# A two-stage transformer kernel: row gathers in loops with listed indices, and row products that read the tokens from PSUM

## The chip, the cores and the metric

One core of one Trainium2 chip runs the whole program. The metric is the device time of one execution in microseconds (us), given as the median of several runs. Everything is computed in float32.

## The reference, cut to what matters

Two blocks run one after the other on 256 tokens of width 1024. The first has two layers of attention and a wide MLP. The second has two layers, each a mixer (sparse attention "nsa", then forgetting attention "fox") and a feed-forward made of experts that are single rows:

```python
def peer_ffn(x, w_q, sub_keys, u, v):
    # 8 heads; each picks 16 of 128 x 128 experts by two top-16 searches
    ...
    h = jax.nn.gelu(jnp.einsum('ted,td->te', u[ec], xc))
    return jnp.einsum('te,ted->td', gc.astype(h.dtype) * h, v[ec])
```

`u` and `v` have 16384 rows of 1024 numbers. Each token uses 8 x 16 = 128 of them, so `ec` has the shape (tokens, 128). The dot of a token with its row of `u` gives a weight, and the rows of `v` are summed with these weights.

## The kernel before, in words

The tokens lie on the 128 partitions in two tiles, t = 0 and 1. The first block, and the start of the second, are a sequence of stages (`SCHEDULE`) that end about 900 us after the start; their weights stream through a ring of two panels of 2 MB.

The rest of the program is the **gather phase**. It has four windows (`WINDOWS`: layer 0 tile 0, layer 0 tile 1, layer 1 tile 0, layer 1 tile 1), each of 128 slots: a slot is one expert of each of 128 tokens. Four slots make a tick (`SLICE`), so a window has 32 ticks (`TICKS`) and the phase has 128. For every slot:

- GpSimd (POOL) gathers one row of `u` for each partition with an indirect DMA (L2262), 128 rows of 4 KB, into one of eight buffers (`urow`, `RING` = 8), and in the same way one row of `v` into one of eight buffers `vrow`. The loop at L2303 to L2310 is written out: it issues u of tick n + 1, then v of tick n. A gather into a buffer in use waits for the count `u_used` or `v_used` (L2261). The first gather of a piece of experts waits for `routed`, which VectorE steps at L1890.
- VectorE (DVE) multiplies the landed u row with the tokens `xn` and sums the product (`expert_dots`, L1917). The result goes to `hdot`, and `u_used` rises by one.
- ScalarE (ACT) applies the gelu to four dots (L1370), multiplies them by the gates (L1375) and spreads each over a diagonal matrix (L1381).
- TensorE (PE) multiplies this diagonal with the v row and adds it up in PSUM banks 0 and 1 (`expert_slice`, L906), and `v_used` rises by one. At a window's end VectorE adds the two banks to the residual (`fold`, L1926) and normalizes (L1931, L1941).

Beside this, the mixer of the next tile or layer and its routing are computed in small steps. `STAGES` gives each stage the tick at which it begins, and the plans (`nsa_plan`, `fox_plan`, `LATE_ROUTE`) give each step a tick. On each engine a step of tick n stands behind the expert work of tick n, so all orders are fixed by hand. A step that uses PSUM is named by a letter and a number: S (scores, softened by DVE at L1968 and L1973 and made to exponentials by ACT at L1454), P (shares turned by PE, L972), O (shares times values, L981), q, k, v, w (projections, L926), s (key scores). They take the banks 2 to 7 in turn:

```python
return ps[:, 8 - SHADOW_BANKS + NUMBER[key] % SHADOW_BANKS, :]
```

and PE waits before it fills a bank until the step six places earlier has been read (`bank`, L885). The softmax works in a buffer `soft` in `scratch`, with `softT` for its transpose. For tile 0 two batches of four heads have room in it, for tile 1 one (`block_of`: depth 2 or 1), so for tile 1 `soften` waits until the batch before has been turned (L1966).

A head is ranked by DVE in `rank_head` (L1839 to L1867) and the experts are written in `choose` (L1873 to L1890). In the first window the first two heads are ranked before tick 0, and gathers begin once the first is chosen; the others are ranked between the dots of ticks 0 to 6.

## Time and profile before

| | |
|---|---|
| median of 3 runs | 2522.19 us (2518.62 to 2525.67) |
| the profiled execution | 2530.18 us, of which 2528.1 us span |
| granted TensorE clock, mean | 0.931 of full speed |
| busy in the span | PE 2149.1 us, DVE 1415.3, ACT 880.9, POOL 1155.1 |
| moved by DMA | 754.69 MB, 544.05 of them by POOL's queue |

An engine's busy time counts its instructions, not what it waits for. For a gather the POOL's time is that in which it makes the transfer's descriptors; the transfer itself runs on the 16 DMA engines and is counted there. The DMA share of a window is the mean busy share of these engines; GB/s is what they moved.

In a row of a timeline stand the start and the duration in us, the engine, the line, the operation with what it writes and reads, and in brackets how long the engine was idle before and who released it ("issue": nothing that the profile shows; "remote": unknown).

### The profile page before, as it was taken

What the parts mean: (1) busy time and instruction counts of PE and PEld (TensorE: products, weight loads), DVE (VectorE), ACT (ScalarE), POOL (GpSimd) and SP (SyncE); (2) the same over time, 40 slices, a digit from 0 to 9 for tenths busy, and PEclk for the clock granted to TensorE, in tenths of its full rate; (3) what the DMA queues carried; (4) which work ended last, traced back from release to release, by engine and by line L of the source; (5) the groups of instructions that cost most, each with busy time, mean ns of one, the idle gap of its engine ahead of it and who ended that gap; (6) DMA issues with size and microseconds to landing.
All of it is one profiled execution on the core that took longest, in us unless ns stands there. A gap on an engine that the chain in (4) does not pass through costs nothing.

```text
span 2528.1 us, 24194 instructions
## 1 busy us (share of the span) xinstructions
PE 2149.1 (85%) x7260; PEld 1254.8 (50%) x7260; DVE 1415.3 (56%) x2996; ACT 880.9 (35%) x2125; POOL 1155.1 (46%) x1076
## 2 busy tenths in 40 slices
PE   7889999799999876798977998887798898667776
PEld 5667878678876542453433444343345343222232
DVE  3474554554565468674575644486635466674433
ACT  3445444644534321462222252233234223222121
POOL 0100000000000047687667667767667767777765
PEclk9999999899999799899999999998899899988898
DMA  8315545055445389899999999999999999999997
GB/s 302 146 67 183 191 174 186 31 175 195 170 146 204 113 327 353 287 338 405 415 409 371 409 410 344 413 413 398 371 414 342 377 412 368 361 323 369 378 354 299
DMA packets 172681, 754.69 MB, mean 299 GB/s; under 512 B 19184, under 2 KB 19344, under 8 KB 152736
## 3 DMA queue, kind: packets, MB, share of 16 engines
q0 software_dynamic: 148640, 544.05, 56.3%
q1 hardware_dynamic: 21584, 197.14, 21.0%
q10 hardware_dynamic: 2352, 12.24, 1.3%
q8 instruction: 49, 0.80, 0.1%
q14 instruction: 56, 0.46, 0.1%
HBM read 752.28 MB, written 4.22 MB: 299 GB/s over the span
## 4 chain that ended last, share of the span: by engine, by line
PE 51%; POOL 12%; DVE 11%; issue 10%; DMA 9%; ACT 3%; another core or an unknown queue 3%; DVEq 1%; ACTq 0%; POOLq 0%; SPq 0%
PE ps L906 15%; POOL Z L2262 12%; PE ps L651 7%; PE ps L652 7%; PE ps L653 7%; PE ps L926 7%; DMA Z<-v,experts 5%; DVE Z L1917 4%; DMA Z<-u,experts 3%; DMA ring<-panels 1%; PE ps L1046 1%; DVE ring_lo L1748 1%; PE ps L641 1%; PE ps L981 1%
## 5 line engine op out<-in xcount | busy, mean ns | idle before, releaser
L906 PE MATMUL ps<-Z 128*128 128x512 f32 x2048 | 995.7, 642 | 259.7 <-DMA Z<-v,experts 175.8
L906 PEld LDWEIGHTS ps<-Z 128*128 128x128 f32 x2048 | 410.0, 206 | 808.1 <-issue 566.3
L1917 DVE CUSTOM_DVE_ANT_0 Z<-Z,xn 128x1024 f32<-128x1024 f32 x512 | 609.6, 1225 | 311.8 <-DMA Z<-u,experts 256.7
L2262 POOL DMA_INDIRECT Z<-u,experts x512 | 561.9, 1097 | 329.1 <-issue 157.3
L2262 POOL DMA_INDIRECT Z<-v,experts x512 | 569.3, 1112 | 262.8 <-issue 126.0
L1748 DVE TENSOR_TENSOR ring_lo<-ring,ring_hi 128x1024 fp32r<-128x1024 f32 x212 | 247.6, 1221 | 195.1 <-ACT ring_hi L1212 194.8
L926 PE MATMUL ps<-ring,o 128*128 128x512 f32 x560 | 251.9, 602 | 2.7 <-issue 1.9
L651 PE MATMUL ps<-ring_hi,xT_lo 128*128 128x512 f32 x592 | 237.4, 401 | 13.7 <-DVE xT_lo L1796 7.3
L652 PE MATMUL ps<-ring_lo,xT 128*128 128x512 f32 x592 | 233.0, 394 | 0.0
L653 PE MATMUL ps<-ring_hi,xT 128*128 128x512 f32 x592 | 232.8, 393 | 0.0
L1212 ACT CAST ring_hi<-ring 128x1024 fp32r<-128x1024 f32 x212 | 208.9, 1051 | 37.8 <-DMA ring<-panels 35.2
L1370 ACT ACTIVATE hdot<-hdot 128x4 f32<-128x4 f32 x128 | 26.5, 207 | 536.3 <-DVE hdot L1917 328.9
L2251 POOL COPY Z<-pj 128x256 f32 x16 | 6.4, 402 | 413.9 <-ACTq L524 365.8
L1381 ACT ACTIVATE Z<-cst,wslot 128x128 f32<-128x128 f32 x512 | 165.3, 392 | 64.1 <-PE ps L906 31.3
L926 PEld LDWEIGHTS ps<-ring,o 128*128 128x128 f32 x560 | 106.8, 193 | 133.6 <-issue 132.6
L2297 POOL COPY ksc<-pj 128x512 f32<-128x512 f32 x5 | 3.4, 712 | 304.1 <-DVE pj L1836 298.1
L651 PEld LDWEIGHTS ps<-ring_hi,xT_lo 128*128 128x128 f32 x592 | 112.6, 190 | 44.9 <-DVE ring_lo L1748 9.4
L653 PEld LDWEIGHTS ps<-ring_hi,xT 128*128 128x128 f32 x592 | 112.6, 190 | 23.9
L652 PEld LDWEIGHTS ps<-ring_lo,xT 128*128 128x128 f32 x592 | 112.8, 191 | 22.9 <-issue 0.5
L1375 ACT ACTIVATE wslot<-hdot,gate_w 128x1 f32<-128x1 f32 x512 | 109.6, 285 | 9.1 <-issue 0.3
L651 PE MATMUL ps<-ring_hi,hT 128*128 128x512 f32 x256 | 100.5, 393 | 1.7 <-DVE hT L1756 1.5
L1389 ACT COPY scratch<-ps 128x512 f32<-128x512 f32 (+1 forms) x70 | 38.5, 568 | 180.4 <-PE ps L926 82.8
(262 smaller groups left out, 2025.6 us busy)
## 6 DMA issues: line engine op xcount, KB each, us to landing
ring<-panels SPq DMA_DIRECT2D x106, 1024.0 KB, 5.0
ring<-panels SPq DMA_DIRECT2D x40, 2048.0 KB
Z<-u,experts POOLq DMA_INDIRECT x512
Z<-v,experts POOLq DMA_INDIRECT x512
gain<-gains ACTq DMA_DIRECT2D x4, 1024.0 KB, 4.5
pj<-keys ACTq DMA_DIRECT2D x4, 1024.0 KB
bias_lines<-bias_line POOLq DMA_DIRECT2D x1, 3072.0 KB, 17.2
gain<-gains ACTq DMA_DIRECT2D x5, 512.0 KB, 3.6
```

Of the source, the lines that this page charges most:

```text
L651: mm(out, b, c, start=start, stop=False)
L652: mm(out, a, d, start=False, stop=False)
L653: return mm(out, a, c, start=False, stop=stop)
L906: last = mm(ps[:, c, :], diag[s], vrow[s][:, c * NC:(c + 1) * NC], start=slot == 0, stop=slot == SLOTS - 1)
L926: last = mm(to, tokT[:, k, :], w[:, k * NC:(k + 1) * NC], start=k == 0, stop=k == KT - 1)
L1212: copy(ring_hi[:, slot, c * CH:(c + 1) * CH], ring[:, slot, c * CH:(c + 1) * CH]).then_inc(hi_ready, 1)
L1375: f(own[:, s:s + 1], cols[:, s:s + 1], ACT.Copy, scale=gate_w[:, t, slot + s:slot + s + 1])
L1381: f(diag[n % RING], ident, ACT.Copy, scale=own[:, s:s + 1]).then_inc(diag_ready, 1)
L1389: copy(to, src).then_inc(act_emptied, 1)
L1748: v.tensor_tensor(ring_lo[:, slot, at], ring[:, slot, at], ring_hi[:, slot, at].bitcast(F32), ALU.subtract).then_inc(lo_ready, 1)
L1917: v.tensor_tensor_reduce(out=urow[s], in0=urow[s], in1=xn[:, t, :], scale=1.0, scalar=0.0, op0=ALU.mult, op1=ALU.add, accum_out=hdot[:, t, ...
L2262: g.indirect_dma_start(out=rows[s], out_offset=None, in_=tables[layer], in_offset=bass.IndirectOffsetOnAxis(ap=experts[:, t, slot:slot + 1 ...
```

## The change

Four things change; the arithmetic is the same.

1. The u dots read the tokens from PSUM. At the start of each window DVE copies the tile's tokens into banks 6 and 7 (`dotted`), and L1917 takes them from there as its second operand.
2. The steps beside the gathers therefore have four banks (2 to 5), from the end of the "middle" stage on; that stage keeps six. For tile 1, `ksc` gives a second buffer for `soft` and `softT`, so that both tiles have depth 2.
3. DVE copies the four indices of each tick into one of four short lists (`listed`), two ticks ahead, behind the dots (`list_rows`). From the fifth tick on it first waits for the v rows that used the list before. Gathers read the lists instead of `experts`, and wait for `rows_listed` instead of `routed`.
4. POOL issues the first four ticks written out (`first_rows`), and then runs a loop whose body is 32 gathers, for four ticks of u and of v. The loop makes 15 turns for each layer, with one such body written out between the two, where u comes from layer 1 and the first v still from layer 0. In these 992 gathers each wait is an instruction of its own (`apart`), against a value computed from the loop's register.

The diff, cut to its core:

```diff
...
-SHADOW_BANKS = 6
+FRONT_BANKS, SHADOW_BANKS = range(2, 8), range(2, 6)
...
+N_MIDDLE = sum(key[0] == "middle" for key in ORDER)
+BANK = [FRONT_BANKS[n % len(FRONT_BANKS)] if n < N_MIDDLE else SHADOW_BANKS[n % len(SHADOW_BANKS)]
+        for n in range(len(ORDER))]
...
+LISTS, LISTED_AHEAD = 4, 2
...
+        listed = sb("listed", [P, LISTS, SLICE], U32)
...
+        dotted = ps[:, 6:8, :]
...
-            return ps[:, 8 - SHADOW_BANKS + NUMBER[key] % SHADOW_BANKS, :]
+            return ps[:, BANK[NUMBER[key]], :]
...
-            t = 0 if key[0] in ("middle", "fox0") else 1
-            return t, int(key[1][1]), (1, 2)[t == 0]
+            return 0 if key[0] in ("middle", "fox0") else 1, int(key[1][1]), 2
...
+            n = BATCH * (t + 1) * P
+            a = (soft, ksc_flat[:, 0:BATCH * SEQ])[i % 2] if t == 1 else soft[:, i % 2 * n:]
+            return a[:, 0:n]
...
+        def soft_turned(key):
+            t, i, depth = block_of(key)
+            n = BATCH * (t + 1)
+            a = (softT, over(ksc_flat[:, BATCH * SEQ:], [[P, 2 * BATCH], [1, P]]))[i % 2] if t == 1 else softT[:, i % 2 * n:]
+            return a[:, 0:n]
...
-                n = NUMBER[key]
-                if n >= SHADOW_BANKS:
-                    emptied(pe, ORDER[n - SHADOW_BANKS])
+                last = held_before(NUMBER[key], BANK[NUMBER[key]])
+                if last is not None:
+                    emptied(pe, ORDER[last])
...
             def expert_dots(tick):

                 t = tick // TICKS % TILES
+                if tick == 0:
+                    for b in (6, 7):
+                        emptied(dve, ORDER[held_before(len(ORDER), b)])
+                if tick % TICKS == 0:
+                    dve.drain()
+                    for c in range(2):
+                        v.tensor_copy(dotted[:, c, :], xn[:, t, c * NC:(c + 1) * NC])
+                    dve.drain()
                 for n in range(tick * SLICE, (tick + 1) * SLICE):
                     s, slot = n % RING, n % SLOTS
                     dve.wait_ge(u_landed[s], 16 * (n // RING + 1))
-                    v.tensor_tensor_reduce(out=urow[s], in0=urow[s], in1=xn[:, t, :], scale=1.0, scalar=0.0,
+                    row = over(urow[s], [[NC, 2], [1, NC]])
+                    v.tensor_tensor_reduce(out=row, in0=row, in1=dotted, scale=1.0, scalar=0.0,
                                            op0=ALU.mult, op1=ALU.add, accum_out=hdot[:, t, slot:slot + 1])\
                         .then_inc(u_used, 1)
+
+            def list_rows(tick):
+
+                t, at = tick // TICKS % TILES, tick % TICKS * SLICE
+                if tick >= LISTS:
+                    for n in range((tick - LISTS) * SLICE, (tick - LISTS + 1) * SLICE):
+                        dve.wait_ge(v_landed[n % RING], 16 * (n // RING + 1))
+                v.tensor_copy(listed[:, tick % LISTS], experts[:, t, at:at + SLICE]).then_inc(rows_listed, 1)

...
                     phase()
             steps = Ticks(beside())
             steps.upto(-1)
+            for tick in range(LISTED_AHEAD):
+                list_rows(tick)
             for tick in range(len(WINDOWS) * TICKS):
                 expert_dots(tick)
+                if tick + LISTED_AHEAD < len(WINDOWS) * TICKS:
+                    list_rows(tick + LISTED_AHEAD)
                 steps.upto(tick)
...
-            def gather(rows, tables, there, tick):
-
-                layer, t = WINDOWS[tick // TICKS]
+            def u_rows(layer, tick, place):
+
+                apart(pool, (rows_listed, tick + 1))
+                for b in range(SLICE):
+                    s = (place * SLICE + b) % RING
+                    apart(pool, (u_used, tick * SLICE + (b + 1 - RING)))
+                    g.indirect_dma_start(out=urow[s], out_offset=None, in_=(u0, u1)[layer],
+                                         in_offset=bass.IndirectOffsetOnAxis(ap=listed[:, place, b:b + 1], axis=0))\
+                        .then_inc(u_landed[s], 16)
+
+            def v_rows(layer, tick, place):
+
+                for b in range(SLICE):
+                    s = (place * SLICE + b) % RING
+                    apart(pool, (v_used, tick * SLICE + (b + 1 - RING)))
+                    g.indirect_dma_start(out=vrow[s], out_offset=None, in_=(v0, v1)[layer],
+                                         in_offset=bass.IndirectOffsetOnAxis(ap=listed[:, place, b:b + 1], axis=0))\
+                        .then_inc(v_landed[s], 16)
...
                 for n in range(tick * SLICE, (tick + 1) * SLICE):
-                    s, slot = n % RING, n % SLOTS
                     if n >= RING:
                         pool.wait_ge(u_used if rows is urow else v_used, n - RING + 1)
-                    g.indirect_dma_start(out=rows[s], out_offset=None, in_=tables[layer],
-                                         in_offset=bass.IndirectOffsetOnAxis(ap=experts[:, t, slot:slot + 1], axis=0))\
-                        .then_inc(there[s], 16)
+                    g.indirect_dma_start(out=rows[n % RING], out_offset=None, in_=table,
+                                         in_offset=bass.IndirectOffsetOnAxis(
+                                             ap=listed[:, tick, n % SLICE:n % SLICE + 1], axis=0))\
+                        .then_inc(there[n % RING], 16)

             for (step, arg), meets in zip(SCHEDULE, MEETS):
...
-            for tick in range(-1, len(WINDOWS) * TICKS):
-
-                after = tick + 1
-                if after < len(WINDOWS) * TICKS:
-                    pool.wait_ge(routed, piece_of(after // TICKS, after % TICKS * SLICE))
-                    gather(urow, (u0, u1), u_landed, after)
-                if tick >= 0:
-                    gather(vrow, (v0, v1), v_landed, tick)
+            for tick in range(LISTS):
+                pool.wait_ge(rows_listed, tick + 1)
+                first_rows(urow, u0, u_landed, tick)
+                if tick > 0:
+                    first_rows(vrow, v0, v_landed, tick - 1)
+            turn = TILES * TICKS // LISTS
+            with pool.Fori(1, turn) as i:
+                for k in range(LISTS):
+                    u_rows(0, i * LISTS + k, k)
+                    v_rows(0, i * LISTS + (k - 1), (k - 1) % LISTS)
+            for k in range(LISTS):
+                u_rows(1, turn * LISTS + k, k)
+                v_rows(k > 0, turn * LISTS + k - 1, (k - 1) % LISTS)
+            with pool.Fori(turn + 1, 2 * turn) as i:
+                for k in range(LISTS):
+                    u_rows(1, i * LISTS + k, k)
+                    v_rows(1, i * LISTS + (k - 1), (k - 1) % LISTS)
+            v_rows(1, 2 * turn * LISTS - 1, LISTS - 1)
```


## Rows read from the trace of the kernel before

**Rows 1.** Windows: length, busy PE, PEld, DVE, ACT, POOL (instructions), clock, DMA share, GB/s
```profile
1000.00:1100.00 100.00, 82.62 (x302) 45.55 (x301) 70.92 (x151) 51.63 (x143) 68.25 (x59) 0.88 0.86 304
1100.00:1200.00 100.00, 83.44 (x239) 39.48 (x237) 55.38 (x113) 34.82 (x104) 76.25 (x68) 0.93 0.99 381
1200.00:1300.00 100.00, 89.36 (x244) 42.49 (x245) 62.48 (x178) 27.63 (x87) 67.36 (x64) 0.98 1.02 413
1300.00:1400.00 100.00, 74.77 (x170) 31.72 (x169) 59.75 (x143) 24.62 (x80) 71.00 (x66) 0.89 1.00 385
...
1500.00:1600.00 100.00, 80.06 (x208) 37.75 (x207) 48.65 (x91) 31.49 (x100) 72.81 (x63) 0.90 0.96 368
...
1700.00:1800.00 100.00, 71.68 (x157) 32.35 (x158) 61.58 (x148) 24.43 (x80) 71.22 (x68) 0.84 1.00 386
1800.00:1900.00 100.00, 100.00 (x271) 47.58 (x270) 53.23 (x132) 34.88 (x93) 63.23 (x55) 0.99 1.01 403
1900.00:2000.00 100.00, 87.25 (x283) 45.22 (x281) 53.99 (x99) 39.24 (x115) 72.10 (x64) 0.95 0.93 346
2000.00:2100.00 100.00, 93.62 (x249) 44.03 (x250) 61.44 (x177) 25.76 (x85) 67.67 (x62) 0.95 1.02 411
2100.00:2200.00 100.00, 72.76 (x145) 29.51 (x143) 63.30 (x148) 27.36 (x89) 77.96 (x70) 0.90 0.96 359
2200.00:2300.00 100.00, 68.75 (x130) 27.61 (x131) 63.31 (x144) 22.08 (x78) 74.83 (x66) 0.85 0.93 341
2300.00:2400.00 100.00, 72.44 (x144) 29.22 (x142) 43.20 (x70) 20.89 (x79) 69.99 (x72) 0.90 0.97 371
2400.00:2528.00 128.00, 88.46 (x176) 35.62 (x176) 50.39 (x86) 25.43 (x93) 75.50 (x76) 0.90 0.87 328
```

**Rows 2.** Groups by line: busy us, mean ns | idle before, releaser
```profile
L1917 DVE CUSTOM_DVE_ANT_0 Z<-Z,xn 128x1024 f32<-128x1024 f32 x512 | 609.6, 1225 | 311.8 <-DMA Z<-u,experts 256.7
L2262 POOL DMA_INDIRECT Z<-u,experts x512 | 561.9, 1097 | 329.1 <-issue 157.3
L2262 POOL DMA_INDIRECT Z<-v,experts x512 | 569.3, 1112 | 262.8 <-issue 126.0
```

**Rows 3.** Timeline, 1341 to 1347 us: GpSimd beside VectorE
```profile
1341.77 1.23 DVE L1926 TENSOR_TENSOR h<-ps,h 128x1024 f32<-128x1024 f32 x1 [5.10 <-remote]
...
1342.01 0.94 POOL L2262 DMA_INDIRECT Z<-v,experts  x1 [3.29 <-remote]
...
1343.13 1.23 DVE L1931 CUSTOM_DVE_ANT_0 o<-h 128x1024 f32<-128x1024 f32 x1
1343.25 1.92 POOL L2262 DMA_INDIRECT Z<-u,experts  x1 [0.31 <-issue]
```

**Rows 4.** Timeline, POOL where the gathers begin
```profile
901.82 1.02 POOL L2262 DMA_INDIRECT Z<-u,experts  x1 [113.79 <-DVE experts L1890]
...
923.83 1.18 POOL L2262 DMA_INDIRECT Z<-u,experts  x1 [7.27 <-DVE hdot L1917]
```

**Rows 5.** Timeline, DVE where the gathers begin
```profile
921.82 1.23 DVE L1917 CUSTOM_DVE_ANT_0 Z<-Z,xn 128x1024 f32<-128x1024 f32 x1
...
922.97 1.22 DVE L1917 CUSTOM_DVE_ANT_0 Z<-Z,xn 128x1024 f32<-128x1024 f32 x1
```

**Rows 6.** Chain that ended last: start us, us, what
```profile
2503.93 4.48 DMA Z<-v,experts
```

**Rows 7.** Waits of POOL from 930 us: us in total, times, longest us
```profile
POOL Z L2262 <- DVE hdot L1917: 54.3, 16, 8.1
```

**Rows 8.** Timeline, POOL copies beside a turn of a loop
```profile
95.98 0.39 POOL L2252 COPY Z<-pj 128x256 f32 x1
96.32 0.40 POOL L2251 COPY Z<-pj 128x256 f32 x1
```

**Rows 9.** Waits of DVE from 900 us
```profile
DVE scratch L1968 <- PE ps L972: 23.6, 8, 4.6
```

**Rows 10.** Timeline, DVE among the steps that rank a head
```profile
977.24 0.43 DVE L1851 TENSOR_TENSOR ranks<-ranks 128x256 f32<-128x256 f32 x1 [2.34 <-issue]
```

More of the change, by code:

```diff
@@ L130, with held_before @@
 NUMBER = {key: n for n, key in enumerate(ORDER)}
+N_MIDDLE = sum(key[0] == "middle" for key in ORDER)
+BANK = [FRONT_BANKS[n % len(FRONT_BANKS)] if n < N_MIDDLE else SHADOW_BANKS[n % len(SHADOW_BANKS)]
+        for n in range(len(ORDER))]
+def held_before(n, bank):
+    return max((m for m in range(n) if BANK[m] == bank), default=None)
 def by_dve(key):
@@ L505, in build @@
         routed = sem("routed")
+        rows_listed = sem("rows_listed")
         logits_ready = sem("logits_ready")
@@ L969, in turn_shares @@
                 pe.wait_ge(soft_ready, softened(key))
-                to, at = bank(key), soft_at(key) + BATCH * P * "ab".index(key[1][2])
+                to, at = bank(key), BATCH * P * "ab".index(key[1][2])
                 for j in range(BATCH):
-                    last = tr(to[:, j * P:(j + 1) * P], soft[:, at + j * P:at + (j + 1) * P], ident)
+                    last = tr(to[:, j * P:(j + 1) * P], soft_of(key)[:, at + j * P:at + (j + 1) * P], ident)
                 last.then_inc(bank_filled, 1)
@@ L977, in weigh @@
                 emptied(pe, (key[0], in_batch("P", t, i)[-1]))
-                to, at = bank(key), soft_at(key) // P
+                to = bank(key)
                 for j in range(BATCH):
                     for kb in range(t + 1):
-                        last = mm(to[:, j * HD:(j + 1) * HD], softT[:, at + j * (t + 1) + kb, :], values[j][kb],
+                        last = mm(to[:, j * HD:(j + 1) * HD], soft_turned(key)[:, j * (t + 1) + kb, :], values[j][kb],
                                   start=kb == 0, stop=kb == t)
@@ L1441, in copy_shares @@
                     filled(act, (key[0], f"O{i - depth}"))
-                at = soft_at(key) // P + 4 * "ab".index(key[1][2])
-                copy_bank(key, softT[:, at:at + 4, :], fours(key))
+                at = 4 * "ab".index(key[1][2])
+                copy_bank(key, soft_turned(key)[:, at:at + 4, :], fours(key))
             def soft_exps(stage, i):
@@ L1452, in soft_exps @@
                 for j in range(BATCH):
-                    a = soft[:, at + j * keys_of:at + (j + 1) * keys_of]
+                    a = soft_of(key)[:, j * keys_of:(j + 1) * keys_of]
                     last = f(a, a, ACT.Exp, bias=peaks[i % 2][:, j:j + 1], accum_out=totals[i % 2][:, j:j + 1])
@@ L1963, in soften @@
                 m, heads = "ab".index(key[1][2]), BATCH // 2
-                a = over(soft[:, soft_at(key) + m * keys_of:], [[2 * keys_of, heads], [1, keys_of]])
+                a = over(soft_of(key)[:, m * keys_of:], [[2 * keys_of, heads], [1, keys_of]])
                 if i >= depth:
@@ L2253, in stage_pairs, with first_rows @@
                         last.then_inc(staged, 1)
[L2255 to L2257 removed]
+            def u_rows(layer, tick, place):
[13 more added lines that the diff above has]
+                        .then_inc(v_landed[s], 16)
+            def first_rows(rows, table, there, tick):
                 for n in range(tick * SLICE, (tick + 1) * SLICE):
[L2259 removed]
                     if n >= RING:
                         pool.wait_ge(u_used if rows is urow else v_used, n - RING + 1)
[L2262 to L2264 removed]
+                    g.indirect_dma_start(out=rows[n % RING], out_offset=None, in_=table,
+                                         in_offset=bass.IndirectOffsetOnAxis(
+                                             ap=listed[:, tick, n % SLICE:n % SLICE + 1], axis=0))\
+                        .then_inc(there[n % RING], 16)
             for (step, arg), meets in zip(SCHEDULE, MEETS):
```

6 lines of the change are left out of this document (3 added, 3 removed).

## The prediction

> **What bounds the kernel now.** I read the windows first, then the groups by line, then the timeline of GpSimd beside VectorE, and last the waits.
>
> The kernel has two halves. The change touches only the second, from the first row gather, some 900 us after the start, to the end at 2528.1. In it 1024 gathers bring 512 KB each (128 rows of 4 KB), u and v in turn. The windows [rows 1] show that no engine is full there: PE is busy 69 to 100 us in 100, DVE 43 to 71, POOL 63 to 78. The column to read is the last one. It goes between two levels: 411 to 413 GB/s in four windows (1200, 1400, 1600 and 2000; first and last stand in the rows), where weight panels come beside the gathers, and 304 to 403 in the others. So the DMA engines can take 412, and in the lower windows they are not given enough.
>
> Who gives them too little is in the groups [rows 2]. A gather costs POOL 1097 to 1112 ns and "issue" before it. The timeline [rows 3] says what its floor is: 0.94 us of work and 0.30 us before the next, 1.245 us from start to start, which would be 0.524 MB / 1.245 us = 421 GB/s, just above what DMA takes. But many gathers last up to 1.99 us. Rows 3 show when: the gather at 1342.01 runs wholly beside L1926, a DVE addition of the same 1024 columns that reads one operand from PSUM and one from SBUF, and takes 0.94 us. The next one, at 1343.25, runs beside L1931, a product with a sum that reads SBUF twice, and takes 1.92 us. L1917, the dot of a u row, is of the form of L1931, and there are 512 of them. A gather that meets one waits until it is through. Over 1024 gathers this is 561.9 + 569.3 - 1024 x 0.945 = 163.5 us of POOL [rows 2].
>
> **Part 1: dots with the tokens in PSUM.** The second SBUF operand goes, so a gather should cost 0.945 us always, like the one at 1342.01 [rows 3]. What this is worth is limited in each window by two numbers of rows 1: the POOL time set free (its busy time less count x 0.945), and the room in DMA, 100 us x (1 - GB/s / 412). I take the smaller:
> 1000: 12.5 (room 26); 1100: 7.5 (freed 12.0); 1300: 6.5 (freed 8.6); 1500: 10.7 (freed 13.3); 1700: 6.3 (freed 7.0); 1900: 11.6; 2100: 11.8; 2200: 12.5; 2300: 2.0; 2400 to 2528: 3.7. The four full windows give 0, and 1800 gives 0 because PE is busy 100.00 of it. Sum 85.1 us.
>
> The dot's own length: L1926 takes 1.23 us for 1024 columns with one operand in PSUM, L1917 1.225, so 0. If it did grow by a tenth, 512 x 0.12 = 61 us would fall on DVE, which idles 311.8 us before its dots, 256.7 of them for the very rows [rows 2]; that cover hides most of it. Nothing shorter than 0.94 us stands in any row, so I allow no gain beyond it.
>
> The tokens must be copied to PSUM at four window starts: two copies of 512 columns and two drains. L1926's 1.23 us for 1024 columns bounds a copy from above; with drains I take 2 us each, 8 in all, half of it hidden by rows in flight: 4 us.
>
> **Part 2: index lists and loops.** Each tick DVE copies four indices into a list, after four waits on v rows. Those v rows were issued before the u rows whose dots have just run, so the waits pass at once. No row shows such a copy; it lies between 0 and one dot (1.225 us), nearer to 0: I take 0.5 us with its waits. 128 of them are 64 us of DVE, hidden by the 256.7 us that it waits for u rows. That cover is missing in the first eight ticks, where DVE ranks heads between dots: 4 us.
>
> **Start.** Before, the first gather left at 901.82, as soon as the first experts were written, and POOL then stood idle 7.27 us [rows 4] for the first dot, at 921.82 [rows 5]. Now the list is written where the first dot stood. The first dot needs the copy (0.5), the wake-up of POOL (0.78: the dot at 921.82 ends at 923.05 and the gather it releases starts at 923.83, [rows 4, 5]), 0.94 for the gather and its landing. A landing takes 4.48 us in the last links of the chain [rows 6]. Together 6.7 us, all on the path, since DVE ranks heads and is the slowest there.
>
> **Coarser release.** Before, row n of u waited for dot n - 8 alone. Now a slice of four waits for the list, that is for all four dots of two slices before. When POOL stands at that point, it waits up to 3 x 1.15 + 0.5 = 3.9 us longer (dots start 1.15 us apart, [rows 5]). POOL waited for DVE 16 times, 54.3 us [rows 7]; 16 x 3.9 = 62 us is the most, 0 the least (if the rows in flight cover it). About half of those waits lie in stretches where DMA has a queue: 31 us.
>
> Loop control: each gather gets a separate wait against a register, a semaphore step, and arithmetic. The POOL copies of L2251 and L2252 already run in such a loop, one on each side of a turn, and stand 0.34 us apart [rows 8], with nothing in between. A gather gives the sequencer 1.245 us. I take 0; what it would cost if not hidden is a rival.
>
> **Part 3: four banks, two soft buffers.** In a tick of attention for tile 1 five steps fill a bank (Sa, Sb, O, Pa, Pb), so PE's fifth waits for the first to be read by DVE. DVE mostly stands waiting for PE at that place, as rows 9 show, so this is near 0. On the other side, DVE no longer waits until the previous batch is turned: L1968 waited for PE L972 8 times, 23.6 us [rows 9]. A third of that reaches POOL: +8 us. Bounds: -24 (the last rival) to +24.
>
> **Sum.** 85.1 - 4 - 4 - 6.7 - 31 + 8 = 47.4 us. The profiled execution took 2530.18 us (span 2528.1), so 2482.8; it lies 8.0 above the median of the three runs, 2522.19, so **2475 us**.
>
> A limit from elsewhere: the Trainium skill, "DMA: Bandwidth & Descriptors", section Bandwidth, says that one core's share of HBM is about 358 GB/s and binds for loads. By it the windows would have no room and the sum would be a loss of about 38 us. The trace disagrees with 413 GB/s over 100 us [rows 1], and the measurement decides.
>
> **Rivals.**
> - *The freed time comes whole* (0.17). The release costs nothing because a faster POOL keeps a deeper queue. 85.1 + 8 - 14.7 = 78, and more where room exceeds what was freed (1000, 1900, 2200): 2425 to 2445.
> - *Gathers alone cannot reach 412* (0.10). The DMA share is 0.93 to 1.00 in windows of 341 to 386 GB/s too [rows 1]; perhaps scattered rows are slower than panels. With 386 as ceiling the 85.1 fall to about 54 (1000: 12.5; 1100 and 1300: 1.6; 1500: 4.7; 1700: 0; 1900: 10.4; 2100: 7.0; 2200: 11.7; 2300 and 2400: 5.7), less the same 38 us of costs: 16 us gained, 2506, and up to 2530 when the costs run high, as no queue of rows covers them here: mostly 2515 to 2525. Against it: 385 and 386 are also just what the POOL gives at 1.49 to 1.52 us per gather.
> - *The loop's control shows between gathers* (0.10), the slower side. If a separate wait is passed only when the gather ahead has left, the 0.78 us of a wake-up [rows 4, 5] stand in place of 0.30. On the 992 gathers issued this way that is up to 476 us. It decides from 0.05 us per gather on, 47 us over 992: above that the kernel is slower. Likely size if it happens: 0.06 to 0.15 us, 2535 to 2625. Against it stand the copies, 0.34 us apart across a turn [rows 8]. A variant is one code load per turn of the loop: DVE stands "issue" 2.34 us in a row of small instructions at 977.24 with nothing to wait for [rows 10]; 30 turns x 2.34 = 70 us, which gives 2545. The Trainium skill, "Runtime: NRT & Kernel Launch", section Instruction fetch mechanics, says that a taken branch to a place outside the two loaded blocks forces a fetch. By that rule it hangs on the length of the body, 32 gathers with their waits, which no row here shows.
> - *Four banks hold PE up* (0.03): a stall of 2 us in each of some 12 ticks with five banks, 24 us, and POOL waits for v slots: 2500.
>
> **How the numbers follow.** The forecast's own range is 2455 to 2505, with 0.60. About 0.3% (7.6 us) is what a measurement of this kernel can tell from no change. Faster: 0.58 of the forecast's 0.60 (the rest for its upper edge), 0.17 and 0.03 of the first and last rivals: 0.78. Same: that edge, 0.02, and 0.08 of the second rival. Slower: 0.10 of the third and 0.02 of the second. The range takes in the first rival's likely part, the second, and the near edge of the third: 2425 to 2530.
>
> **What would show it.** Right: gathers of 0.94 us on average (POOL busy near 970 us, not 1131), no gather of 1.99 us beside a dot, windows 2100 to 2400 near 385 to 405 GB/s, the first gather after 922, POOL's wait for DVE up from 54 to 80 or 100 us, dots still 1.22 us. Wrong: gathers still of 1.9 us; gaps of 0.4 us or more between gathers with no releaser; windows without panels that stay below 390 GB/s while POOL stands waiting for used slots.

## The result and the profile after

The changed kernel takes 2579.68 us (median of 4 runs, 2570.94 to 2588.15) against 2520.40 of the kernel before beside it: a ratio of 1.0234 [1.0194, 1.0274], 59 us slower, where 47 us faster was predicted. In a later session it gave 1.0227 [1.021, 1.0244]. On a chip on which the kernel before itself takes only 2451.54 us, the same kernel was 0.9917 [0.9901, 0.9934], 18 us **faster**. Both belong to the result. The experiments below explain the loss; why that chip turns it into a gain stays open in part.

The groups by line of the kernel after (profiled execution 2588.15 us, span 2586.0), which answer to [rows 2]:

```profile
L1949 DVE CUSTOM_DVE_ANT_0 Z<-Z,ps 128x1024 f32<-128x1024 f32 x512 | 607.7, 1219 | 293.6 <-DMA Z<-u,listed 227.6
L2305 POOL DMA_INDIRECT Z<-u,listed x496 | 475.7, 959 | 342.7 <-DVE listed L1959 189.2
L2314 POOL DMA_INDIRECT Z<-v,listed x500 | 474.7, 949 | 310.3 <-issue 141.9
```

The gathers fell from 1097 to 1112 ns to 949 to 959, and the dots kept their length. Beside a dot a gather now takes 0.94 us, where [rows 3] had 1.92. Two dots in VectorE's timeline of the kernel after:

```profile
1345.34 1.22 DVE L1949 CUSTOM_DVE_ANT_0 Z<-Z,ps 128x1024 f32<-128x1024 f32 x1
...
1346.48 1.22 DVE L1949 CUSTOM_DVE_ANT_0 Z<-Z,ps 128x1024 f32<-128x1024 f32 x1
```

and the gathers beside them, in GpSimd's:

```profile
1345.92 0.94 POOL L2314 DMA_INDIRECT Z<-v,listed  x1 [2.88 <-remote]
1347.16 0.94 POOL L2314 DMA_INDIRECT Z<-v,listed  x1 [0.30 <-issue]
```

So the first step of the forecast holds: POOL got its time back (busy 1001.6 us, before 1155.1). But it could not use it. The windows, in the columns of [rows 1]:

```profile
1000.00:1100.00 100.00, 69.89 (x226) 35.34 (x225) 66.78 (x163) 38.07 (x110) 55.78 (x57) 0.85 0.80 295
1100.00:1200.00 100.00, 75.55 (x255) 39.49 (x253) 53.91 (x122) 38.08 (x105) 49.97 (x54) 0.86 0.75 284
1200.00:1300.00 100.00, 90.01 (x210) 40.47 (x211) 43.83 (x100) 25.87 (x84) 57.06 (x60) 0.91 1.02 413
...
2200.00:2300.00 100.00, 66.20 (x128) 27.15 (x127) 66.11 (x199) 21.31 (x74) 60.20 (x63) 0.85 0.92 338
2300.00:2400.00 100.00, 68.97 (x140) 28.05 (x138) 52.61 (x93) 25.48 (x88) 64.87 (x69) 0.90 0.95 362
```

The window from 1100 had 68 gathers and 381 GB/s, and now has 54 and 284. The two late ones shown, which were to rise to 385 or more, stay at 338 and 362 (the one from 2100 rose from 359 to 380). POOL stood waiting instead. Its waits from 930 us on (us in total, times, longest us), which answer to the one row of [rows 7]:

```profile
POOL Z L2305 <- DVE listed L1959: 189.2, 34, 11.7
POOL Z L2305 <- issue: 148.5, 449, 3.8
POOL Z L2314 <- issue: 141.9, 419, 3.5
POOL Z L2314 <- remote: 85.0, 25, 5.5
POOL Z L2314 <- PE ps L929: 80.6, 47, 4.2
```

The 189.2 us for the lists stand where 54.3 us for dots stood before. "issue" is mostly the 0.30 us ahead of every gather. One of the long waits, first in VectorE's timeline:

```profile
1104.77 0.69 DVE L2008 SCALAR_TENSOR_TENSOR scratch<-ps,cst 128x512 f32<-128x512 f32 x1 [6.36 <-remote]
...
1107.42 1.22 DVE L1949 CUSTOM_DVE_ANT_0 Z<-Z,ps 128x1024 f32<-128x1024 f32 x1
...
1110.84 1.22 DVE L1949 CUSTOM_DVE_ANT_0 Z<-Z,ps 128x1024 f32<-128x1024 f32 x1
...
1111.98 0.17 DVE L1959 COPY listed<-experts 128x4 uint32<-128x4 uint32 x1
```

and in GpSimd's:

```profile
1100.45 0.94 POOL L2314 DMA_INDIRECT Z<-v,listed  x1 [0.30 <-issue]
1113.12 0.94 POOL L2305 DMA_INDIRECT Z<-u,listed  x1 [11.73 <-DVE listed L1959]
```

DVE is held up for 6.36 us at a soften of the attention beside ("remote": the trace does not say by whom), then does four dots, and only then copies the list. A gather that waits for its slot alone goes when the first of those dots is done, at 1108.6; this one goes at 1113.12. Meanwhile 11.7 us pass without a new row, and the DMA engines run dry. In the columns of [rows 1], the last 6 us of the wait are:

```profile
1107.00:1113.00 6.00, 5.45 (x34) 3.57 (x33) 5.91 (x14) 5.74 (x17) 0.00 (x0) 1.00 0.01 3
```

They moved 3 GB/s there.

### The profile page after: what moved, and what is told of

Its sections match the earlier page's. It is cut to its first block, busy times and chain, and to the rows that moved or that the text cites. A ratio compares the mean times of both kernels' runs of the same rounds, so it can differ in the third digit from the quotient of the medians.

```text
span 2586.0 us, 26357 instructions
## 1 busy us (share of the span) xinstructions
PE 2161.2 (84%) x7260; PEld 1258.0 (49%) x7260; DVE 1427.4 (55%) x3132; ACT 880.2 (34%) x2125; POOL 1001.6 (39%) x1076
## 4 chain that ended last, share of the span: by engine, by line
PE 41%; issue 15%; DVE 14%; DMA 11%; POOL 8%; another core or an unknown queue 5%; ACT 3%; DVEq 2%; POOLq 1%; ACTq 0%; SPq 0%
PE ps L929 9%; PE ps L674 7%; PE ps L675 7%; PE ps L676 7%; DMA Z<-v,listed 7%; DVE Z L1949 6%; PE ps L949 5%; POOL Z L2305 4%; POOL Z L2314 3%; DMA Z<-u,listed 3%; DMA ring<-panels 1%; PE ps L1069 1%; DVE ring_lo L1771 1%; PE ps L664 1%
## 5 line engine op out<-in xcount | busy, mean ns | idle before, releaser
L929 PE MATMUL ps<-Z 128*128 128x512 f32 x2048 | 1009.3, 648 | 288.0 <-DMA Z<-v,listed 155.3
L1949 DVE CUSTOM_DVE_ANT_0 Z<-Z,ps 128x1024 f32<-128x1024 f32 x512 | 607.7, 1219 | 293.6 <-DMA Z<-u,listed 227.6
L2305 POOL DMA_INDIRECT Z<-u,listed x496 | 475.7, 959 | 342.7 <-DVE listed L1959 189.2
L2314 POOL DMA_INDIRECT Z<-v,listed x500 | 474.7, 949 | 310.3 <-issue 141.9
L674 PE MATMUL ps<-ring_hi,hT 128*128 128x512 f32 x256 | 100.4, 392 | 1.6 <-DVE hT L1779 1.5
L676 PE MATMUL ps<-ring_hi,hT 128*128 128x512 f32 x256 | 99.7, 390 | 0.0
```

What stands on the lines that cost most here:

```text
L674: mm(out, b, c, start=start, stop=False)
L676: return mm(out, a, c, start=False, stop=stop)
L929: last = mm(ps[:, c, :], diag[s], vrow[s][:, c * NC:(c + 1) * NC], start=slot == 0, stop=slot == SLOTS - 1)
L1949: v.tensor_tensor_reduce(out=row, in0=row, in1=dotted, scale=1.0, scalar=0.0, op0=ALU.mult, op1=ALU.add, accum_out=hdot[:, t, slot:slot + 1])\
L2305: g.indirect_dma_start(out=urow[s], out_offset=None, in_=(u0, u1)[layer], in_offset=bass.IndirectOffsetOnAxis(ap=listed[:, place, b:b + 1] ...
L2314: g.indirect_dma_start(out=vrow[s], out_offset=None, in_=(v0, v1)[layer], in_offset=bass.IndirectOffsetOnAxis(ap=listed[:, place, b:b + 1] ...
```

## The experiments

The ratios are against the kernel before of the same session, which took 2511 to 2522 us except where noted. There were five such sessions, on four chips; the chip of the first measurement is not on record.

**Banks and soft buffers alone.** The changed kernel without lists, without loops, and with the dots from SBUF:

```diff
-SHADOW_BANKS = 6
+FRONT_BANKS, SHADOW_BANKS = range(2, 8), range(2, 6)
...
-            return t, int(key[1][1]), (1, 2)[t == 0]
+            return 0 if key[0] in ("middle", "fox0") else 1, int(key[1][1]), 2
```

> The kernel before with four banks and two soft buffers alone; the dots read SBUF, gathers as before. Theory A: within 10 us of before, 2510 to 2530. Rival B: 2550 or more.

2511.03 us, 0.9996 [0.9967, 1.0025], as theory A has it. Part 3 costs nothing.

**PSUM dots with them.** The same with the dots of the change; the gathers read `experts` as before.

```diff
-                    v.tensor_tensor_reduce(out=urow[s], in0=urow[s], in1=xn[:, t, :], scale=1.0, scalar=0.0,
+                    row = over(urow[s], [[NC, 2], [1, NC]])
+                    v.tensor_tensor_reduce(out=row, in0=row, in1=dotted, scale=1.0, scalar=0.0,
```

> The changed kernel with the lists and the loops taken out: gathers written out as before, reading experts, each waiting for one slot; the dots still read PSUM, four banks, two soft buffers. Theory A (the loss is the list: POOL waits for four dots and a copy instead of one dot, 189 us behind L1959 now): POOL's waits fall back to about 54 us behind DVE and the time to 2450 to 2500 us, below the kernel before. Rival B (the four banks and the faster POOL make PE and DVE wait for each other): the time stays at 2550 to 2580.

2500.19 us, 0.9966 [0.9941, 0.999], and 0.9952 [0.993, 0.9973] in a session on another chip. So the PSUM dots gain 11 us over the kernel just above. The time lies at the upper edge of theory A, and the waits for dots came to 103.8 us and not to 54. The groups and waits of both say where the rest stays. The groups of GpSimd with dots from SBUF (kernel with banks alone):

```profile
L2293 POOL DMA_INDIRECT Z<-u,experts x512 | 549.6, 1073 | 338.3 <-issue 150.6
L2293 POOL DMA_INDIRECT Z<-v,experts x512 | 557.6, 1089 | 268.9 <-issue 123.6
```

its waits from 930 us on:

```profile
POOL Z L2293 <- PE ps L929: 111.7, 108, 4.6
POOL Z L2293 <- DVE hdot L1940: 66.3, 16, 6.5
POOL Z L2293 <- remote: 33.7, 17, 3.4
```

The groups with dots from PSUM:

```profile
L2302 POOL DMA_INDIRECT Z<-u,experts x512 | 484.4, 946 | 374.1 <-issue 153.5
L2302 POOL DMA_INDIRECT Z<-v,experts x512 | 487.7, 953 | 349.4 <-PE ps L929 158.3
```

and its waits:

```profile
POOL Z L2302 <- PE ps L929: 158.3, 115, 4.0
POOL Z L2302 <- DVE hdot L1949: 103.8, 49, 9.0
POOL Z L2302 <- remote: 48.3, 20, 4.1
```

The gathers shrink by 1107.2 - 972.1 = 135.1 us, and the waits for used slots, those with an unknown releaser ("remote") among them, grow by 310.4 - 211.7 = 98.7 us. The slots of a ring of eight are given back by the dots and by PE's products, and the waits show that these came hardly sooner for a quicker POOL. What sets their pace on these chips was not tested; the two experiments on it further down ran on another chip.

**The list ahead of the dots.** One line moved: the list of tick n + 2 is copied before the dots of tick n.

```diff
+                if tick + LISTED_AHEAD < len(WINDOWS) * TICKS:
+                    list_rows(tick + LISTED_AHEAD)
                 expert_dots(tick)
-                if tick + LISTED_AHEAD < len(WINDOWS) * TICKS:
-                    list_rows(tick + LISTED_AHEAD)
```

> The changed kernel with one edit: the list of tick n + 2 is written before the dots of tick n instead of behind them, so u gathers are again released row by row. Loops and separate waits stay. Theory A: most of the loss goes, 2480 to 2520. If the loop and its separate waits cost the time (rival C): 2560 to 2580, no change.

2534.77 us, 1.0104 [1.0059, 1.0149]: 31 to 33 us of the 59 gone, less than theory A had and far more than rival C. POOL now waits 98.1 us for dots (37 times) and for lists hardly at all.

**The first lists early too.** The first two lists behind the first choice of experts, not where the first dot stood.

```diff
                             choose(t, lo, hi)
+                            if window == 0 and piece == 0:
+                                dve.drain()
+                                for k in range(LISTED_AHEAD):
+                                    list_rows(k)
```

> The kernel with the list ahead of the dots (2535 us) and, besides, the first two lists written right behind the first choice of experts, so that the first gathers leave at about 900 us and not 920. Theory A (the late start costs 18 us: 8 to the first dot and 10 while the pipeline fills): 2510 to 2520. If the start is hidden by the ranking of heads: no change, 2535.

2521.00 us, 1.0037 [1.0015, 1.0059], and 1.0012 [0.9985, 1.0039] on another chip. The first gather starts at 897.2 in place of 920.3 us, and the first dot at 918.7 in place of 926.4. The end moves by 17 to 23 us, more than the first dot's 7.7, of which 3.2 are not due to the edit: in this execution the first experts, too, were written that much earlier (896.5 against 899.75). The 2521.00 us are just above theory A's range.

**The lists alone.** The kernel before with lists and loops (six banks, dots from SBUF).

```diff
+                if tick + LISTED_AHEAD < len(WINDOWS) * TICKS:
+                    list_rows(tick + LISTED_AHEAD)
...
-                                         in_offset=bass.IndirectOffsetOnAxis(ap=experts[:, t, slot:slot + 1], axis=0))\
+                                         in_offset=bass.IndirectOffsetOnAxis(ap=listed[:, place, b:b + 1], axis=0))\
```

> The kernel before with lists and loops alone; six banks, dots from SBUF, so gathers are blocked up to 1.99 us as before. Theory A: slower than the changed kernel, 2600 to 2640, since blocked gathers and coarse waits add up. Rival B: about as before, 2520 to 2540.

2553.39 us, 1.0155 [1.0096, 1.0215], and 1.019 [1.0133, 1.0248] on another chip: 39 to 48 us, between the two expectations. Lists and loops lose without the other parts, so most of the loss is theirs. POOL waits 148.2 us for lists.

**The lists written but not read.** The kernel without lists, with DVE copying all 128 of them behind their waits for v rows.

> The kernel without lists and loops (2500 us) with the list copies and their waits for v rows put back on VectorE, read by nobody: the gathers do not wait for them. It prices VectorE's added work alone. Theory A (hidden by its waits for rows): 2500 to 2507. If the copies or their waits for landed v rows hold the dots up: 2510 or more.

2500.72 us, 0.9953 [0.9927, 0.9978], as theory A has it: no cost. A copy takes 0.17 us. What costs is that POOL waits for it.

**The loops written out.** The changed kernel with its 992 gathers in a row, each with its wait on itself; the lists stay. The edit takes out two things at once, the loops and the separate waits against a register.

```diff
-            with pool.Fori(1, turn) as i:
-                for k in range(LISTS):
-                    u_rows(0, i * LISTS + k, k)
+            for tick in range(-1, len(WINDOWS) * TICKS):
+                    first_rows(urow, (u0, u1)[...], u_landed, after)
```

> The changed kernel with the loops written out: gathers still read the lists and wait for them behind the dots, but each wait is fused into its gather and no branch is taken. If the loop's control costs nothing (theory A): as the changed kernel, within 10 us, about 2570. If it costs (rival C): 30 us or more faster.

2545.49 us, 1.0143 [1.009, 1.0196]: 23 us better by the ratios, between the two expectations. Run again in the last session, with an expectation that named the loops:

> The changed kernel with its loops written out, once more, order of the lists as in the change. Theory (the loops cost some 20 us): 1.012 to 1.017 where the changed kernel is 1.023. Rival (the first value was a chance): 1.020 to 1.026. If the call falls on the undisturbed chip, where the changed kernel is 0.992: 0.984 to 0.988 by the theory, 0.990 to 0.994 by the rival.

2553.86 us, 1.0137 [1.0108, 1.0166], as the theory has it. And the early lists with the loops written out:

> The list first and the first two lists early, and GpSimd's gathers written out, each with its wait for the used slot on the gather itself, rows still read from the lists. Theory (the loops cost the rest): 0.995 to 0.998 of the kernel before, as without lists. Rival (GpSimd still cannot pass a list that VectorE has not copied, and this is the rest; the loops cost nothing): 1.000 to 1.005, as with the loops.

2507.28 us, 0.9949 [0.9922, 0.9975], as without lists. So the loops with their separate waits cost 21 to 24 us in the changed order and 16 to 22 in the early one. The gathers in the loops stand 0.30 us apart, and the first gather of a turn has a median of 0.31 us ahead of it, in the changed kernel and in the one with early lists. So the gaps do not show the cost, and where these microseconds arise was not found.

**The changed kernel with dots from SBUF.**

> The changed kernel with the dots reading SBUF again: lists, loops, four banks and two soft buffers stay. If PSUM dots help with lists too: slower than the changed kernel, 2580 to 2600. If a faster POOL only finds the list sooner (the same wait, met earlier): 2560 to 2575, equal. It also tells whether the four banks cost anything once lists are there, against lists and loops on six banks (2553).

2548.72 us, 1.0137 [1.009, 1.0184]. That is lower than the changed kernel with its PSUM dots (1.0227 to 1.0234), and lower than both expectations. With lists behind the dots the PSUM dots gained nothing and cost 23 to 24 us by these ratios, where they gain 11 without lists. Why was not found; the kernel with lists alone, at 1.0155 and 1.019, lies between. POOL waited 123.1 us for lists 23 times, against 189.2 and 34.

**Half the products.** To see whether PE's return of v slots is what takes the freed time, two kernels without lists leave out the second half of each expert product's columns, one with each kind of dot. The next two, the six slots and the changed kernel ran beside them on one chip, the one where the kernel before takes 2451.54 us.

```diff
-last = mm(ps[:, c, :], diag[s], vrow[s][:, c * NC:(c + 1) * NC],
+last = mm(ps[:, c, 0:NC // 2], diag[s], vrow[s][:, c * NC:c * NC + NC // 2],
```

> The kernel without lists (PSUM dots, four banks), but each expert product covers only the first half of its columns, so the second half of each expert's output is left out: TensorE's work between two v rows halves. Beside it runs the same cut with the SBUF dots. Theory: the PSUM dots free GpSimd some 150 us, which comes back as waits for v slots because TensorE returns them no faster; with half the products the waits for TensorE fall well under 100 us, and the PSUM dots are worth 30 to 85 us against the other one. Rival: the gathers are bound by the landing rate (about 405 GB/s in windows without panels) whatever frees the slots: both kernels end within 15 us of each other.

> The same cut (expert products of half their columns, the other half left out) with the dots that read the tokens from SBUF, four banks. Theory: GpSimd is the bound here, its busy time near 1150 us stays, and the time is 30 to 85 us above the one with PSUM dots. Rival: within 15 us of it.

PSUM dots 2411.88 us, SBUF dots 2431.40: 19.5 us, between the theory's 30 to 85 and the rival's 15. The waits of the one with PSUM dots:

```profile
POOL Z L2302 <- PE ps L929: 149.6, 137, 5.9
POOL Z L2302 <- DVE hdot L1949: 110.6, 90, 9.0
```

and of the one with SBUF dots:

```profile
POOL Z L2293 <- PE ps L929: 79.3, 102, 5.4
POOL Z L2293 <- DVE hdot L1940: 55.8, 18, 4.9
```

The gathers shrank by 1093.8 - 970.3 = 123.5 us, and the waits for slots grew by 125.1 ("issue" fell by 21.5, since the 0.30 us ahead of a gather that waits are counted with its wait). The theory had said that the waits for TensorE fall well under 100 us with half the products; they are 149.6. So the length of PE's products is not what takes the freed time here. The window 2200 to 2300 of the one with SBUF dots shows what does in it:

```profile
2200.00:2300.00 100.00, 58.76 (x154) 44.55 (x153) 48.58 (x79) 21.00 (x81) 76.52 (x78) 0.74 1.03 409
```

409 GB/s with the slow gathers already, and 409 with the quick ones: in this window the transfers are the bound, and the waits for slots are their shadow. Not in all of them: the quick gathers carry 408 GB/s against 379 in the window from 2100, 413 against 401 from 1100, and 369 against 349 from 1000. There the pace of POOL still counts on this chip.

**Six slots.** The kernel without lists, each gather waiting for the row six before it.

```diff
-                    if n >= RING:
-                        pool.wait_ge(..., n - RING + 1)
+                    if n >= RING - 2:
+                        pool.wait_ge(..., n - RING + 3)
```

> The kernel without lists (PSUM dots, four banks) with each gather waiting until the row six before it is used, in place of eight: rings of six slots in effect. Theory (slots come back late, so fewer rows in flight is the bound): waits for used slots grow over 300 us in sum and the time is 40 us or more above 2500. Rival (the DMA queues' rate alone is the bound and slot waits are its shadow): under 15 us slower.

2448.63 us, 0.9988 [0.9978, 0.9998]. The waits for slots are 311.2 us from 930 us on, over 300 as expected, but the kernel with eight slots had 310.4 on another chip, 48.3 of them with an unknown releaser. Its expectation was written for a chip at 2511 us, and the kernel with eight slots was not measured on this one, so what two slots are worth stays open.

**The changed kernel on that chip.**

> The changed kernel again, beside the other kernels of this call on one chip: about 2565 to 2590 us. It fixes the scale for the unrolled kernel and the one with SBUF dots: if it stays 1.02 of the kernel before or more, both of those (1.014) were faster than it; if it comes at 1.014, neither loops nor PSUM dots cost anything there.

2433.16 us, 0.9917 [0.9901, 0.9934], which the expectation did not have. Its windows reach what was forecast for them, and more:

```profile
1000.00:1100.00 100.00, 89.19 (x351) 49.28 (x352) 81.01 (x177) 60.14 (x164) 66.42 (x70) 0.93 0.94 358
1100.00:1200.00 100.00, 84.65 (x221) 39.68 (x221) 51.87 (x105) 30.19 (x99) 67.92 (x72) 0.90 1.02 409
...
2200.00:2300.00 100.00, 73.05 (x155) 30.53 (x156) 47.49 (x86) 23.33 (x90) 75.61 (x81) 0.95 1.03 409
```

The change alone does not bring these: on this chip the kernel with half products and SBUF dots had 401 and 409 GB/s in the last two of these windows already, and the kernel before was not profiled here.

The instructions are the same as on the other chips. A difference shows in idle time that no releaser explains. DVE's waits "issue" among the rank operations from 930 us on, the largest of the kernel after in its first measurement:

```profile
DVE ranks L1885 <- issue: 21.2, 9, 4.1
DVE ranks L1878 <- issue: 18.4, 9, 4.1
DVE ranks L1882 <- issue: 12.1, 9, 3.0
DVE ranks L1890 <- issue: 11.3, 7, 2.9
```

and the largest on this chip:

```profile
DVE ranks L1887 <- issue: 0.7, 2, 0.4
DVE ranks L1874 <- issue: 0.4, 1, 0.4
```

These operations follow one another on DVE's own results and wait for nobody. Over all groups on `ranks` from 930 us on "issue" is 95 us there and 2 here; "remote", over all of DVE, is 172 us there and 0 here. The kernel before, in its own profile, has 57 us of "issue" there ([rows 10] is one of them). The single list copy and the drains of the change cannot be their cause, since they are the same on both chips. In VectorE's timeline of the kernel after (first measurement) six such idle times, 11.2 us in all, stand between two groups of dots some 15 to 28 us into the gathers. Two of them, and the list that stands behind them:

```profile
937.16 0.09 DVE L1882 MATCH_VALUE_LOAD ranks<-ranks 128x8 f32 x1 [2.31 <-issue]
...
941.41 0.43 DVE L1885 MAX8 ranks<-ranks 128x8 f32<-128x256 f32 x1 [3.37 <-issue]
...
950.96 0.17 DVE L1959 COPY listed<-experts 128x4 uint32<-128x4 uint32 x1
```

GpSimd's timeline has the gather that waits for it:

```profile
951.40 0.94 POOL L2323 DMA_INDIRECT Z<-u,listed  x1 [8.55 <-DVE listed L1959]
```

On the chip without such stalls the same gather goes out without a wait. But the lists hold POOL up on that chip too: its waits for them from 930 us on are

```profile
POOL Z L2305 <- DVE listed L1959: 144.1, 49, 7.5
```

against 189.2 us in 34 waits. The stalls make single waits longer. But the 45 us between the two sums are less than the 77 between 59 us slower and 18 us faster.

**The order of the variants again.** The changed kernel, the one without lists, the one with early lists and the lists alone once more, to see whether the ratios hang on the chip.

> The changed kernel once more. Theory (its cost is that GpSimd waits for a list that stands behind VectorE's other work, and is large only where VectorE itself is held up): 1.015 to 1.03 of the kernel before if that one takes about 2510 us and DVE shows over 100 us of idle time without a releaser or with an unknown one, 0.99 to 0.995 if that one takes about 2450 us and DVE shows none. Rival (the first measurement was a chance of one session): near 0.992 on either.

> PSUM dots and four banks with the gathers written out from the rank table. Where the kernel before takes 2510 us: 0.996 again. Where it takes 2450 us: by the theory that slots come back sooner on the undisturbed chip, the PSUM dots bring more, 2415 to 2430 us (0.985 to 0.992); by the rival that the transfers are the bound there already, within 5 us of the kernel before.

> The changed kernel with the list of the tile after next ahead of the dots and the first two lists right behind the first choice. Where the kernel before takes 2510 us: 1.004 again, some 50 us under the changed kernel. Where it takes 2450 us: only the late start of 20 us is left to gain, 2410 to 2420 us, 15 to 25 us under the changed kernel.

> The kernel before with the lists and the loops alone (dots from SBUF, six banks). Where the kernel before takes 2510 us: 1.016 again. Where it takes 2450 us: theory, the late start is most of what is left, 2465 to 2475 us (1.006 to 1.01); rival (the coarser release costs the same 35 us everywhere): over 2485 us.

All four ran on a chip with stalls (before 2521.88 us), and gave 1.0227, 0.9952, 1.0012 and 1.019, near what each expectation says for such a chip. The groups on `ranks` show 79 us of "issue" in the changed kernel there. The rival, that the first measurement was a chance of one session, falls. What the one without lists, the one with early lists and the lists alone do on the chip without stalls was not measured.

## Why the prediction was wrong

Where the kernel before takes 2511 to 2522 us, the parts add up like this, each from a pair of kernels that differ in it alone (1 us is 0.0004; "loops" holds their separate waits too; kernels of different sessions are set against each other by their ratios, so each line is uncertain by some 8 us; the two lines in the middle make 39 together):

```
banks and soft buffers    0.9996                      -1 us
PSUM dots, no lists       2511.0 -> 2500.2            -11
loops                     0.9949 -> 1.0012, 1.0037    +16 to +22
first lists late          1.0012, 1.0037 -> 1.0104    +23 to +17
list behind the dots      1.0104 -> 1.0234, 1.0227    +31 to +33
DVE's work on the lists   0.9966 -> 0.9953            0
sum                                                   +58 to +60; measured +59
```

The lines are steps of one way from the kernel before to the changed one, so their sum has to come out near the measured 59 and proves nothing; each line stands on its own pair. The price of a part also hangs on which others are there: the PSUM dots gain 11 us without lists and cost 23 to 24 with lists behind the dots.

The forecast was 47.4 us faster, so it missed by 106. Of these, 70 lie in part 1 with its copies (81.1 against 11), 16 to 22 in the loops, 10 to 16 in the start and 7 in part 3; the lists gave 4 back.

- **Part 1, 85.1 us: the step that failed.** The mechanism was right, the unblocked gather as well, and its price of 0.94 us. The room was misread. I took "what DMA could still carry" in a window as something that POOL alone keeps from it. But rings of eight slots stand between POOL and DMA, and of 135 us set free, 99 came back as waits for used slots. [rows 2] and [rows 7] had warned of it: DVE already waited 256.7 us for u rows while POOL waited 54.3 us for DVE, so each waited for the other in turn, and neither was the bound alone. A row of the same view that was left out had more. In the kernel before POOL waited for slots of v, too:

```profile
POOL Z L2262 <- PE ps L906: 99.4, 97, 4.6
```

The room is smaller in the other column, too. In [rows 1] the DMA share is 0.96 and 0.93 in the windows from 2100 and 2200, against 1.02 in the full ones. That leaves 6 and 9 parts in a hundred, not the 13 and 17 that GB/s gave. Worked out from that column, part 1 would be some 54 us (an estimate), still five times what it measured. The smaller of "freed" and "room" is an upper bound, not an estimate. Part 1 measured 11 us, about an eighth. What gives the slots back no sooner on these chips stays open.
- **Coarser release, -31 us.** It measured 31 to 33. The number held by luck: I had 3.9 us for each of 16 waits, halved. There were 34 waits, of up to 11.7 us, because everything that holds DVE ahead of the dots, an attention step or a stall, now holds the next slice too.
- **Start, -6.7 us.** From the first experts written to the first dot it took 26.7 us (897.53 to 924.26), before 20.5 (901.36 to 921.82): 6.3 more, near the 6.7 worked out. But between the two orders of the first lists the end moved by 17 to 23 us. I had counted only the first dot. Before, POOL issued its first rows 20 us ahead of it; now the next slices, too, hang on DVE at its slowest place. That this makes up the rest is argued, not shown.
- **Lists, -4 us.** 0. The copy is 0.17 us, not 0.5.
- **Loop control, 0.** A second step that failed: 16 to 24 us. My ground for nothing was a misreading. I said that the copies of [rows 8] stand one on each side of a turn. A turn of that loop makes four copies, and these are the second and third of the first turn (it starts at 95.64); every other turn starts after a wait for another engine, so no row of the kernel before shows what a turn costs. The rival had it at 0.06 us per gather or more, and asked for gaps between gathers. The cost measured is 0.02 us per gather, below the 0.05 from which I said it decides, and the gaps of the loop are not where it lies: 892 of the 1023 gaps are 0.29 to 0.32 us. It is half a hit of the rival's direction by another way.
- **Part 3, +8 us.** 0, inside its bounds. The rival of four banks falls with it.
- **Gathers alone cannot reach 412.** They carried 409 GB/s in the window from 2200 on the chip without stalls, so scattered rows are no slower than that. On a chip like that of the forecast the PSUM dots without lists carried 403 in the window from 1300, above the 386 of the rival. What I had as the other explanation for 341 to 386, POOL's own pace, was a part of it only: in the windows from 2100, 2200 and 2300 the kernel with banks alone had 344, 352 and 362 GB/s, and with PSUM dots 365, 371 and 361.
- **The sign on the two kinds of chip.** I read [rows 10], 2.34 us of "issue" among small operations, as a price for a code load and put it in a rival. It is one of the stalls that VectorE shows at irregular places on this chip, and that no profile taken on the chip at 2451 us has in this size (0.4 us at most in the changed kernel). That the lists turn such stalls into waits of POOL is seen in the rows above. That they make the change 18 us faster on the one chip and 59 slower on the others is not shown: POOL waits 144.1 us for lists on the chip without stalls as well, and the variants between were not run there. The forecast of 2475 is 0.981 of its base, and no full kernel reached that on any chip.

Of the signs of "wrong" under "what would show it", one came true to the letter: windows without panels that stay below 390 GB/s while POOL stands waiting for used slots.

## What to carry to other kernels

Before a producer's freed time is counted as gain, ask who gives its slots back and whether he was already waiting: with rings between engines that wait for each other in turn, time freed on one side can return as a wait on the other, here 99 of 135 us. Whatever is put between a producer and its slots as a batched permission (here a list of four, behind four dots) inherits all delays of the engine that writes it, so write it first and far ahead, not behind other work: that one line was worth 31 us here, and with the first lists early and the loops written out the lists were free. Take the parts that gain and leave the others: on the chips at 2511 to 2522 us the best full kernels are the PSUM dots without lists, 0.9952 to 0.9966 of the kernel before, and the one with early lists and no loops, 0.9949, which are the same within the noise.

## What the runs showed of the hardware

- The same program runs at 2451 us on one chip and at 2511 to 2522 on the others, and within one session the runs of a kernel lie within 1.3%. Nearly the whole difference arises once the row gathers run: in two kernels without lists the first dot comes at 918.3 us on the one chip and at 918.7 on another. On the slower chips PE, DVE and ACT show 46 to 453 us each of idle time "issue" from 900 us on, on the faster one 5 us at most. What holds them is not known. The faster chip moved more while they were absent, 409 GB/s in the window from 2200 against 338 for the same kernel.
- A ratio of 1.023 on one chip and 0.992 on another, each with an interval of a third of a per cent: the interval of a session says nothing about the next chip. A change like this one should be measured on more than one.
- What each engine would look like beside a dot was as forecast. The Trainium skill, "SBUF — State Buffer", section "SBUF: two separate sides", says that a VectorE operation with two SBUF inputs and a GpSimd operation that reads SBUF exclude each other for a whole instruction. The traces agree: 0.94 us for a gather beside dots from PSUM, 1.92 beside an operation that reads SBUF twice ([rows 3]). The runs add that the 135 us of POOL time freed by it were worth 11 us here.
- The DMA engines carried 409 GB/s over 100 us with gathers alone. The Trainium skill, "DMA: Bandwidth & Descriptors", section Bandwidth, has about 358 GB/s for each core where both cores of an HBM domain stream; whether a neighbour streamed in any of these sessions no trace here shows.
